# Seven half-size products (Strassen's scheme, Winograd's form) in place of eight, in a one-core fp32-accurate decoder layer

## What is computed

```python
hn = rmsnorm(x, norm_g)                     # x: 2048 tokens x 1024
proj = hn @ w_in                            # 1024 -> 3584 columns: u, v, z_a, h, gb, gc, z_b of 512 each
out_a = spatial_gating(u, v, ...) * silu(z_a)      # layernorm of v; per head a causal 128x128 mix of tokens
out_b = gb * causal_conv3(gc * h) * silu(z_b)
x1 = x + concat(out_a, out_b) @ w_out       # 1024 x 1024
gate = sigmoid(rmsnorm(x1, ple_norm_g) @ w_ple_gate)    # 1024 x 1024
x2 = x1 + gate * (p @ w_ple_proj)           # 256 -> 1024
out = rmsnorm(x2, final_g)
```

## Time and profile before

| | |
|---|---|
| time, 3 runs | 1085.88 us median (1084.97 to 1086.48) |
| span of the profiled execution (first to last instruction) | 1084.5 us; its own time outside the span is not recorded, the median of the runs is 1.4 us above the span |
| PE busy | 1053.2 us, 4838 matmuls |
| DVE, ACT busy | 597.3 us, 391.3 us |
| mean granted TensorE clock | 0.995 of full |
| bytes moved | 126.23 MB, mean 116 GB/s |

### The profile page before, as it was taken

How to read it: one execution, slowest core, us unless ns; L and a number is a source line. 1 busy time by engine, 2 the same in 40 slices (tenths; PEclk the granted TensorE clock), 3 DMA queues, 4 the chain that set the end, 5 groups by cost and what they waited for, 6 DMA issues and landing times.

```text
span 1084.5 us, 13403 instructions
## 1 busy us (share of the span) xinstructions
PE 1053.2 (97%) x4838; PEld 876.2 (81%) x4838; DVE 597.3 (55%) x984; ACT 391.3 (36%) x567; POOL 6.9 (1%) x11
## 2 busy tenths in 40 slices
PE   4999999999999999999999999999999999999994
PEld 3888888888888888888888888888888888888883
DVE  6456565456475654554657566554566555553455
ACT  4323322355433222335443323233544232222443
POOL 2000000000000000000000000000000000000000
PEclk9999999999999999999999999999999999999997
DMA  6354332422366322333236533333234553323321
GB/s 184 108 179 151 97 97 79 136 79 97 99 209 198 97 86 90 118 97 97 82 105 212 193 90 97 98 100 114 83 93 127 181 158 97 92 86 95 93 83 77
DMA packets 136258, 126.23 MB, mean 116 GB/s; under 512 B 6272, under 2 KB 107136, under 8 KB 136192
## 3 DMA queue, kind: packets, MB, share of 16 engines
q1 hardware_dynamic: 136192, 125.33, 36.9%
HBM read 116.93 MB, written 8.39 MB: 116 GB/s over the span
## 4 chain that ended last, share of the span: by engine, by line
PE 96%; DVE 1%; DMA 1%; ACT 0%; SPq 0%; issue 0%; DVEq 0%; ACTq 0%
PE acc L369 31%; PE acc L371 31%; PE acc L370 31%; PE small L423 3%; PE small L490 1%; DMA x_res<-in_x_dram 1%; PE small L491 0%; DVE x_res L906 0%; ACT square L535 0%; DVE newton L724 0%; DVE x_res L856 0%; DVE v_raw L854 0%; ACT gate L621 0%; SPq L297 0%; DVEq L144 0%
## 5 line engine op out<-in xcount | busy, mean ns | idle before, releaser
L693 DVE TENSOR_TENSOR w_lo<-w_raw,w_hi 128x1024 fp32r<-128x1024 f32 x150 | 183.8, 1225 | 322.6 <-ACT w_hi L528 322.6
L528 ACT ACTIVATE w_hi<-w_raw 128x1024 fp32r<-128x1024 f32 x152 | 161.1, 1060 | 430.6 <-PE acc L371 420.7
L369 PE MATMUL acc<-hn_hi,w_hi 128*128 128x512 f32 x768 | 299.7, 390 | 0.0
L370 PE MATMUL acc<-hn_lo,w_hi 128*128 128x512 f32 x768 | 298.8, 389 | 0.0
L371 PE MATMUL acc<-hn_hi,w_lo 128*128 128x512 f32 x768 | 298.8, 389 | 0.0
L371 PEld LDWEIGHTS acc<-hn_hi,w_lo 128*128 128x128 f32 x768 | 144.2, 188 | 30.0
L370 PEld LDWEIGHTS acc<-hn_lo,w_hi 128*128 128x128 f32 x768 | 144.2, 188 | 29.5
L369 PEld LDWEIGHTS acc<-hn_hi,w_hi 128*128 128x128 f32 x768 | 144.2, 188 | 29.3
L369 PE MATMUL acc<-w_hi,mix_hi 128*128 128x512 f32 x256 | 101.3, 396 | 0.0
L369 PE MATMUL acc<-w_hi,x_hi 128*128 128x512 f32 x256 | 101.0, 395 | 0.0
L371 PE MATMUL acc<-w_hi,mix_lo 128*128 128x512 f32 x256 | 99.9, 390 | 0.0
(11 more groups left out here) (97 smaller groups left out, 1065.9 us busy)
## 6 DMA issues: line engine op xcount, KB each, us to landing
w_raw<-in_w_in_dram SPq DMA_DIRECT2D x112, 512.0 KB, 3.7
w_raw<-in_w_out_dram SPq DMA_DIRECT2D x32, 512.0 KB, 4.0
w_raw<-in_w_ple_gate_dram SPq DMA_DIRECT2D x32, 512.0 KB, 3.7
x_res<-in_x_dram SPq DMA_DIRECT2D x4, 2048.0 KB, 8.7
out_dram<-x_res SPq DMA_DIRECT2D x16, 512.0 KB, 5.7
x_in<-in_x_dram SPq DMA_DIRECT2D x12, 512.0 KB, 4.1
w_raw<-in_w_ple_proj_dram SPq DMA_DIRECT2D x8, 512.0 KB, 3.8
x_res<-in_x_dram SPq DMA_DIRECT2D x4, 512.0 KB, 6.0
```

Source lines behind the costliest of these rows:

```text
L369: pe.matmul(ps, left_hi, right_hi, start=first, stop=False)
L370: pe.matmul(ps, left_hi, right_lo, start=False, stop=False)
L528: ins = act.activation(w_hi[:, u % 2, :], w_raw[:, u % 2, :], ACT.Copy)
L693: ins = dve.tensor_tensor(w_lo[:, u % 2, :], w_raw[:, u % 2, :], w_hi[:, u % 2, :].bitcast(F32), ALU.subtract)
```

## The change

Tokens are now worked in 2 blocks of 1024. Each product C = A B with A (tokens x 1024) and B (1024 x columns) is cut in two along each of its three dimensions. With A11..A22 and B11..B22 the quarters, seven products are formed instead of eight, in this order (`q` = 0 to 6):

A11 B11; A12 B21; S2 T2; S1 T1; S3 T3; S4 B22; A22 T4, where S1 = A21 + A22, S2 = S1 - A11, S3 = A11 - A21, S4 = A12 - S2, and T1 = B12 - B11, T2 = B22 - T1, T3 = B22 - B12, T4 = B21 - T2.

Products 0, 2, 4, 6 accumulate in one PSUM bank (`IN_A`), products 1, 3, 5 in another, which products 1 and 3 open anew (`OPENS`). Three readings by ACT (`copy_v`, `copy_t`, `copy_g`: after q = 0, 2, 3) and three additions by DVE (`add_v`, `add_t`, `add_natural`: after q = 1, 4, 5) make C11, C12, C22 in SBUF; C21 is what stands in the first bank after q = 6. In the O product x takes the place of the copies (`add_x`, L1293, x read once more in quarters). P keeps its plain form.

Each S is made by DVE from raw transposed operands (`sum_op`), each T from raw weights in place (`sum_w`), and each product's operands are then split as before: `split_op`/`low_op` for A11, A12, S2, S1, S3, S4, A22 (`slots`), `split_w`/`low_w` into a ring of 4 places of 512 columns. A T product reads 512 columns of weights, so it has one ring place and 12 matmuls; T has 12 groups of 7 products (4 A groups: z_a,u; then H: h,gate_c and Z: gate_b,z_b in turn). V's columns are now cut in halves of 256, and so are its matmuls: 128x256. O and G products have 48 matmuls of 512 columns in two halves (`kk`) of 24, each with two ring places.

norm_g is applied by ACT when it copies the transposed x (`raw_x`), not by DVE. x1 is stored to a DRAM tensor `x1_dram` after O, G's copies and sigmoids take its place in `keep`, and it is read back tile by tile in P (`x1_again`). The weights' `lo` in the first two units is no longer made by POOL.

```diff
-BLOCKS = seq // HALF
+BLOCKS, TILES, KC, HEADS = 2, 8, 8, 4
+A11, A12, S2, S1, S3, S4, A22 = range(7)
+IN_A = (True, False, True, False, True, False, True)
+OPENS = (True, True, False, True, False, False, False)
+RING = 4
...
+            def group(b, g, q):
+                a, bb = 4 + 2 * (g % 2), 5 + 2 * (g % 2)
...
+                elif q == 2:
+                    pe.wait_ge(bank_copied, COPIED("T", b, g, P1))
+                elif q == 3:
+                    pe.wait_ge(bank_added, ADDED("T", b, g, "c11"))
+                elif q == 4:
+                    pe.wait_ge(bank_copied, COPIED("T", b, g, U2))
+                elif q == 5:
+                    pe.wait_ge(bank_copied, COPIED("T", b, g, P5))
+                else:
+                    pe.wait_ge(bank_added, ADDED("T", b, g, "c22"))
+                pe.wait_ge(w_lo_ready, W_LO("T", b, g, q))
...
+                for c in range(4):
+                    ins = three_of(banks[:, a if IN_A[q] else bb, :], hi[:, c, :], lo[:, c, :], op_hi(q)[:, c, :], op_lo(q)[:, c, :],
+                                q, c)
...
+            def natural(b, stage, q, kks, operand, columns):
...
+                    pe.wait_ge(op_lo_ready, OP_LO(operand, b, q, kk))
...
+            pe.wait_ge(ident_ready, 1)
+            for b in range(BLOCKS):
+                if b == 0:
+                    x_fills(0, "A11")
+                    x_fills(0, "A12")
+                    spatial_weights()
+                for q in range(PRODUCTS):
+                    natural(b, "V", q, (0, 1), "hn", 256)
+                    if b == 0 and q == 0:
+                        x_fills(0, "A21")
+                        x_fills(0, "A22")
...
+                if name == "T1":
...
+                    ins = dve.tensor_tensor(q11, q12, q11, ALU.subtract)
+                elif name == "T2":
...
+                    ins = dve.tensor_tensor(t2_view(stage), q22, q11, ALU.subtract)
+                elif name == "T3":
+                    ins = dve.tensor_tensor(q12, q22, q12, ALU.subtract)
+                else:
...
+                    ins = dve.tensor_tensor(q21, q21, t2_view(stage), ALU.subtract)
...
+                if s == S1:
...
+                    ins = dve.tensor_tensor(out_, a21, a22, ALU.add)
...
+            def add_t(b, g, q):
+                which, name, bank = {1: (P1, "c11", 5), 4: (P5, "c22", 4), 5: (U2, "c12", 5)}[q]
+                dve.wait_ge(product_done, PRODUCT("T", b, g, q))
+                dve.wait_ge(bank_copied, COPIED("T", b, g, which))
+                t = temp(g, which)
+                dve.tensor_tensor(t, banks[:, bank + 2 * (g % 2), :], t, ALU.add).then_inc(bank_added, ADDED.up("T", b, g, name))
...
+                for i in range(TILES):
+                    sp.wait_ge(bank_added, ADDED("O", b, "c12", i) if i < 4 else ADDED("O", b, "x", 1, 0, i - 4))
+                    sp.dma_start(x1_tiles[b, i], nat(i)).then_inc(x1_stored[i], 16)
```

More of the change, by code:

```diff
@@ L71, in unit_of @@
[L71 to L118, removed]
+BLOCKS, TILES, KC, HEADS = 2, 8, 8, 4
+A11, A12, S2, S1, S3, S4, A22 = range(7)
+PRODUCTS = 7
+IN_A = (True, False, True, False, True, False, True)
+OPENS = (True, True, False, True, False, False, False)
@@ new lines, with ring_place @@
+RAW_SLOT = {"A11": S2, "A12": S4, "A21": S3, "A22": A22}
+QUARTERS = {"A11": (0, 0), "A12": (0, 1), "A21": (1, 0), "A22": (1, 1)}
+GROUPS = [("A", h) for h in range(HEADS)]
+for _i in range(HEADS):
+    GROUPS += [("H", _i), ("Z", _i)]
+GROUP_COLUMNS = {"A": ("z_a", "u"), "H": ("h", "gate_c"), "Z": ("gate_b", "z_b")}
+NG = len(GROUPS)
+MIX_AFTER = {(2, 2): 0, (2, 6): 1, (3, 3): 2, (4, 2): 3}
+RING = 4
+V0, T0, O0, G0, P0, RING_BLOCK = 0, 14, 98, 126, 154, 158
+def ring_place(b, stage, *at):
+    x = {"V": lambda p: V0 + 2 * p, "T": lambda g, p: T0 + PRODUCTS * g + p,
+         "O": lambda p, kk: O0 + 4 * p + 2 * kk, "G": lambda p, kk: G0 + 4 * p + 2 * kk,
+         "P": lambda kp: P0 + 2 * kp}[stage](*at)
+    return (b * RING_BLOCK + x) % RING
@@ L344, in _, with constants @@
+            for i in range(TILES):
+                sp.wait_ge(out_stored[i], BLOCKS * 16)
+                sp.wait_ge(x1_stored[i], BLOCKS * 16)
+        def constants(pool):
             pool.memset(warm[:, 0:1], 0.0).then_inc(pool_set, 1)
@@ L358, in _, with products, three @@
             pool.wait_ge(w_s_landed, 16)
-            wsn = uz[:, 0, :].rearrange("t (h s) -> t h s", h=heads)
             pool.affine_select(out=wsn, in_=wsn, compare_op=ALU.is_ge, fill=0.0, base=0,
                                pattern=[[0, heads], [-1, P]], channel_multiplier=1).then_inc(masked, 1)
-        @block.tensor
-        def _(pe):
-            def product(ps, left_hi, left_lo, right_hi, right_lo, first, last):
-                pe.matmul(ps, left_hi, right_hi, start=first, stop=False)
+        def products(pe):
+            def three(ps, left_hi, left_lo, right_hi, right_lo, opens, closes):
+                pe.matmul(ps, left_hi, right_hi, start=opens, stop=False)
@@ new lines, in spatial_weights @@
+            def spatial_weights():
+                pe.wait_ge(masked, 1)
+                for h in range(heads):
+                    ins = pe.transpose(banks[:, 4, h * P:(h + 1) * P], wsn[:, h, :], ident[:, :])
+                ins.then_inc(wst_done, 1)
+                pe.wait_ge(wst_lo_ready, 1)
+                pe.matmul(banks[:, 5, :], ones_r[:, :], wst[:, :, 0, :], start=True, stop=False)
+                pe.matmul(banks[:, 5, :], ones_r[:, :], wst[:, :, 1, :], start=False, stop=True).then_inc(wst_done, 1)
@@ L915 @@
+        for program in (products, scalar_program, vector_program):
+            program(Rehearsal())
+        for count in counts:
+            count.settle()
+        block = ctx.enter_context(nc.Block())
+        block.sync(loads)
+        block.gpsimd(constants)
+        block.tensor(products)
+        block.scalar(scalar_program)
+        block.vector(vector_program)
 _INS = ["x", "p", "norm_g", "w_in", "ln_v_g", "ln_v_b", "w_s", "b_s", "conv_w", "w_out", "ple_norm_g",
```

1907 lines of the change are left out of this document (1267 added, 640 removed).

## The result

The changed kernel takes 1077.86 us (median of 4 runs, 1076.67 to 1081.11), the one before 1086.18 (4 runs, 1084.97 to 1086.91): ratio 0.9931, 95% interval 0.9915 to 0.9948. It is 0.7% faster where 2.9% were forecast. The right sign, a quarter of the size.

The account below looks back on a forecast made before the run. PE was taken to bound the kernel (busy 1053.2 of 1084.5 us). New PE work 930.0 plus 123 idle made a span of 1053, with 1.4 between span and median 1055; the 8-in-10 range was 1022 to 1092.

Parts of the forecast that it names:

- O: Stage O, both blocks: 76.1 us of PE against 65 of DVE, a half product ahead, so 2 us idle.
- G: Stage G: DVE's work badly spread, PE waits for operands and weights; 13.2 us idle in one block, 11.6 in the other.
- PE's work: Matmuls, transposes and mixes of the whole kernel: 930.0 us after the change, 117.8 less than before.
- rival 3: V's 256-column matmuls: loads do not overlap, 0.226 us each, 1129 us in all; decides from 0.161 per matmul; chance 0.06.
- Start: Kernel start through first V: chains and DVE delay the products, V ends at 87 us; costs 41 in place of 21.
- P and V of the second block: First P and next V: V's first weights late on DVE, 13.7 us wait, then 3 + 2; 18.4 in all.
- End: Last P and after: DVE's chains and y tiles take 21.7 us after P's work, where 15.3 stood.
- The clock: PE's slow restarts after idleness: 1.7 us three times, twice at the start, once at second-block V; 5 us.
- rival 4: PE's clock: 25 slow restarts after short waits cost 42 us, 1097 in all; decides from 18 restarts; chance 0.07.
- Rival 2: DVE is the bound: full durations and ACT-DVE semaphore hops count at every step; 1075 to 1090 us; chance 0.15.
- Rival 1: Stalls are smaller: T, O, G and second-block V terms shrink by half (29 us), 1015 to 1035 us; chance 0.17.
- The likeliest case: Whole kernel: the forecast itself, 1055 us, by itself 1038 to 1073, with chance 0.55.

Follow-up runs that it names:

- experiment 8: Against the changed kernel, stage O's weight sums T1 to T4 taken over one column only, the rest left out: 1065.81 us, ratio 0.9814.
- 10: Against the changed kernel, eight useless 128x1024 DVE subtractions added in O's first half: 1088.1 us, ratio 1.0021.
- 11: Against the changed kernel, the same eight useless DVE subtractions added in O's second half, in product 5: 1079.11 us, ratio 0.9927.
- 12: Against the changed kernel, in O alone DVE's next weight sums and lo parts put ahead of the additions out of PSUM: 1072.83 us, ratio 0.9874.
- 4: Against the changed kernel, the second block's first V weights put ahead of x's operands in the ACT and DVE queues: 1081.25 us, ratio 0.9949.
- 7: Against the changed kernel, the second block's x scaled by ACT instead of DVE: 1079.61 us, ratio 0.9936.
- Experiment 5: Against the changed kernel, three waits of PE (two in the first V, one ahead of the second) filled with useless matmuls: 1078.31 us, ratio 0.9921.

## Why the prediction was half right

**The failed step is O**: "76.1 us of PE, 65 of DVE, a half product ahead: 2 for both blocks together." It measured 21.2. The step divided one stage's DVE work by the stage's length, which four lines further on, for G, it refused to do ("The work is badly spread"). O is as badly spread: between 340 and 385 us DVE has eleven `lo` parts of operands, the operand sums, seven of the block's eight sums of weights and two rounds through ACT; between 385 and 418 it has `lo` parts of weights and additions. Experiments 8, 10 and 11 show that it is the amount of work in that half, and 12 that part of it can be moved out. How the remaining 4.0 of idle after experiment 8 divides between the round trips through ACT and the operand sums was not tried.

**PE's work**: 932.7 instead of 930.0. V's matmuls of 256 columns start 0.120 us apart, where I took 0.116: 80.6 us for 672, not 78.0. That the loads overlap with the columns is right, so rival 3's condition did not hold; the 117.8 us of gained work are 115.1. **DVE** is busy for 818.5 us, between the 888 of full durations and the 800 that I thought nearer.

**Start**: product 0 forecast at 34, 1 at 47, 2 at 59, T at 87; measured 34.5, 49.0, 61.5, 93.0. The sum (44.8 against 44.4 with the clock) is right. Of the 6 us by which T is late, 2.5 are product 2's later start, 0.8 V's interval (240 matmuls of 0.120 for 5 products, 28.8 where I had 28) and 2.8 the slow matmuls behind product 2's wait; 3.4 of the 6 stood in the forecast under the clock.

**T**: 6.4 and 6.3, where I had 5 for each, and in the places named (the first two groups), with one wait of 1.05 in the last group.

**G**: 12.8 and 10.4 for 13.2 and 11.6; the wait for S2's `lo` ahead of product 2 was forecast at 4.2 and is 4.41.

**P and V of the second block**: forecast 13.7 of wait at V's first weights, measured:

```profile
562.88 0.58 PE L407 MATMUL banks<-ring_hi,slot 128*128 128x256 f32 x1 [14.04 <-DVE ring_lo L1048]
```

Experiments 4 and 7 say that neither its order nor x's scaling is what to change there.

**End**: 19.1 us behind the last matmul and 4.4 of waits in the last P, for 21.7. The last matmul and the last row scale:

```profile
1056.96 0.39 PE L402 MATMUL banks<-ring_hi,slot 128*128 128x512 f32 x1
```

```profile
1071.83 1.28 DVE L1331 SCALAR_TENSOR_TENSOR keep<-keep,rstd,final_b 128x1024 f32<-128x1024 f32 x1
```

**The spill costs nothing**, as forecast. The whole wait of anything for x1's way back is

```profile
DVE keep L1324 <- DMA side<-x_dram: 0.3, 1, 0.3
```

**The clock**: I counted 5 us for three restarts; the slow matmuls are 34.2 us against 5.2 before, on the way to the 42 that rival 4 gave for 25 restarts. Half clock came back after waits of 3.90 us in V and of 2.73 in O; after 1.74 in T (at 122.65) it did not. The Trainium skill (TensorE: Matmul & The Clock Gate, "HAM oscillation — how this bites in real kernels") says that bursts of matmuls with waits between them keep a kernel returning to half clock; the trace agrees.

But the time that rival 4 gave did not come, and the mean granted clock stayed at 0.966, above the 0.95 that I had named as its sign. Outside O the slow matmuls are 22 us more than I had counted for the clock, and the waits 20 us less than forecast, so most of them took the place of waiting. Not all did. Experiment 5 shows both cases in V: nothing is lost in product 1, 1.4 us are paid behind product 2. And the changed kernel's own runs get longer as their clock gets lower (1076.67 us at 0.967, 1081.11 at 0.959). In O, where the slow matmuls are 7.5 us, PE was not kept busy in the waits in any run, so whether they cost anything by themselves there stays open; that they go when the waits go (1.2 and 1.3 left in experiment 8) is shown.

**The rivals.** Rival 2 (DVE the bound) gave 1075 to 1090, and the time lies in its range, but not for its reason: it asked for waits at every step (8 us more in each T than the 5 forecast), and T has 6.4, G less than forecast. DVE is the bound in one half of one stage, as far as the runs show it. Rival 1 (the stalls are smaller) fell: without PE's work the span has 143.6 us, not 123 or less. The likeliest case's own range ended at 1073; O's 19 us carried the time past it. That the wide range (1022 to 1092) held the time is luck as far as the reason goes: its upper end came from rival 2.

## What to carry to other kernels

When an edit moves work to an engine that had been cover, balance it over the stretch between two points at which PE can wait, not over the stage: here the same eight subtractions cost 10 us or 1, by which half of a stage they stood in. Work that nobody waits for (additions into results) can go behind work that is waited for where slack follows; in G, where none did, the same order lost what O had won. And a saving of an eighth of PE's matmuls pays only where the sums it needs have an engine with time for them: of 115 us saved, 107 went back, in waits at the ends and for operands and weights, and in slow matmuls.

## What the runs showed of the hardware

- Half clock after short waits: after 3.90 us of idleness the matmuls of 256 columns start 0.213 us apart for 4.8 us, then 0.12. It costs nothing where the next operand is late anyway: product 2 starts 12.49 us behind product 1 with it and without. Behind product 2, where no such wait follows, V took 31.56 us with 6 us of half clock and 30.17 with 3.
- With weights loaded for every matmul, 256 columns cost 0.120 us and 512 cost 0.2266: loads and columns overlap, and the narrow form loses only 6% of throughput.
- POOL's two-source subtractions take 1.4 to 1.7 us (512 columns) and 2.7 to 3.1 (1024), 2 to 2.5 times DVE's time. With 136 of them in the kernel DVE's two largest groups of two-source instructions on SBUF take 18 and 30% longer, while those that read PSUM keep their 687 ns.
